# Attention in a hybrid decoder layer: the normalising multiplications of the probabilities on GpSimd instead of VectorE, and one of five value products in full f32 instead of two

## What is computed

```python
def masked_softmax(s, mask):
    s = jnp.where(mask, s.astype(jnp.float32), -jnp.inf)
    m = jnp.max(s, axis=-1, keepdims=True)
    m = jnp.where(jnp.isfinite(m), m, 0.0)
    e = jnp.exp(s - m)
    return e / jnp.maximum(jnp.sum(e, axis=-1, keepdims=True), 1e-30)
...
p_c = masked_softmax(s, cmp_end[None, :] <= t[:, None])
o_c = jnp.einsum('bgrqn,bgnd->bgrqd', p_c.astype(dt), cv)
...
o = (gates[..., 0:1] * unblock(o_c) + gates[..., 1:2] * unblock(o_s)
     + gates[..., 2:3] * unblock(o_w))
```

## Time and profile before

| | us |
|---|---|
| median of 3 runs (lowest, highest) | 1763.86 (1763.45, 1766.72) |
| the profiled execution | 1763.33 |
| its span from the first to the last instruction | 1761.2 |
| TensorE busy, of the span | 1649.9 (94%) |
| VectorE busy | 1049.6 (60%) |
| ScalarE busy | 630.3 (36%) |
| GpSimd busy | 90.7 (5%) |

### The profile page before, as it was taken

The page is one execution under the profiler, slowest core; times in us unless marked ns, Lnnn a source line. Parts: engine busy times, 40 slices in busy tenths (PEclk is TensorE's granted clock), DMA queues, the critical chain, the costliest instruction groups (busy, mean ns, idle before and its releaser), DMA issues.

```text
span 1761.2 us, 22256 instructions
## 1 busy us (share of the span) xinstructions
PE 1649.9 (94%) x8157; PEld 1334.5 (76%) x8157; DVE 1049.6 (60%) x2098; ACT 630.3 (36%) x1177; POOL 90.7 (5%) x126
## 2 busy tenths in 40 slices
PE   8899999997789999989899999999999999997894
PEld 6688888897656767668688888888888888876673
DVE  6734556655899999732555555555555555555233
ACT  5215344345677777621422122122122122113121
POOL 0101211220000000001000000000000000000002
PEclk9899999997899999999999999999999999998997
DMA  5433232234000000230212112112112112102002
GB/s 191 137 97 114 95 116 89 70 120 159 22 16 17 18 4 1 96 108 1 96 38 71 36 36 72 36 36 72 36 36 72 36 36 72 48 0 96 0 36 83
DMA packets 49002, 110.57 MB, mean 63 GB/s; under 512 B 8992, under 2 KB 17184, under 8 KB 48928
## 3 DMA queue, kind: packets, MB, share of 16 engines
q1 hardware_dynamic: 41504, 85.47, 14.8%
q0 software_dynamic: 7424, 24.12, 4.1%
HBM read 89.65 MB, written 19.92 MB: 62 GB/s over the span
## 4 chain that ended last, share of the span: by engine, by line
PE 80%; DVE 9%; ACT 3%; issue 2%; DMA 2%; POOL 0%; POOLq 0%; DVEq 0%; SPq 0%; ACTq 0%
PE ps L1360 28%; PE ps L1035 13%; PE ps L1036 12%; PE ps L1037 12%; PE ps L1181 3%; PE ps L1297 3%; PE ps L1254 2%; PE ps L1260 1%; PE ps L1204 1%; PE ps L1299 1%; DVE htl L1674 1%; PE ps L1040 1%; PE ps L1300 1%; DVE mx L1724 1%; DMA out<-ost 1%
## 5 line engine op out<-in xcount | busy, mean ns | idle before, releaser
L1860 DVE TENSOR_TENSOR h<-h,ps 128x512 f32<-128x512 f32 x352 | 236.4, 686 | 157.0 <-PE ps L1037 155.3
L1360 PE MATMUL ps<-hth,wuh 128*128 128x512 f32 x704 | 218.8, 392 | 3.1 <-DVE wul L1674 3.1
L1360 PE MATMUL ps<-htl,wuh 128*128 128x512 f32 x704 | 218.7, 392 | 0.0
L1360 PE MATMUL ps<-hth,wul 128*128 128x512 f32 x704 | 218.5, 392 | 0.0
L1035 PE MATMUL ps<-wh,xth 128*128 128x512 f32 (+1 forms) x448 | 186.7, 417 | 14.9 <-DVE wl L1456 13.3
L1037 PE MATMUL ps<-wh,xtl 128*128 128x512 f32 (+1 forms) x448 | 170.8, 381 | 0.0
L1036 PE MATMUL ps<-wl,xth 128*128 128x512 f32 (+1 forms) x448 | 170.3, 380 | 0.0
L976 ACT ACTIVATE ffh<-ffa 128x1024 fp32r<-128x1024 f32 x22 | 23.3, 1060 | 385.1 <-DVE ffa L1877 385.1
L1360 PEld LDWEIGHTS ps<-hth,wuh 128*128 128x128 f32 x704 | 132.6, 189 | 33.0 <-issue 3.3
L1360 PEld LDWEIGHTS ps<-hth,wul 128*128 128x128 f32 x704 | 132.4, 188 | 29.3
L1360 PEld LDWEIGHTS ps<-htl,wuh 128*128 128x128 f32 x704 | 132.5, 188 | 28.8
(11 more groups left out here) (263 smaller groups left out, 3155.6 us busy)
## 6 DMA issues: line engine op xcount, KB each, us to landing
wuraw<-in_w_up SPq DMA_DIRECT2D x44, 512.0 KB, 5.3
wraw<-in_w_in SPq DMA_DIRECT2D x48, 256.0 KB, 3.3
proj_d<-stage POOLq DMA_DIRECT2D x48, 256.0 KB, 2.3
wdraw<-in_w_down SPq DMA_DIRECT2D x22, 512.0 KB, 3.5
rin<-proj_d POOLq DMA_DIRECT2D x32, 256.0 KB, 4.3
xraw<-in_xt SPq DMA_DIRECT2D x16, 256.0 KB, 5.8
h<-in_x SPq DMA_DIRECT2D x1, 4096.0 KB, 12.5
owraw<-in_w_out SPq DMA_DIRECT2D x16, 256.0 KB, 3.2
```

The lines of the kernel that those rows point to most:

```text
L1360: mm = nc.tensor.matmul(ps[:, 2 * part + half, :], w_, x_[:, k, half * 512:(half + 1) * 512], start=(k == 0 and i == 0), stop=(k == NK - 1 ...
L1860: nc.vector.tensor_tensor(hh, hh, ps[:, 4 + o_ % 4, :], ALU.add).then_inc(dn_add, 1)
```

## The change

Guard and reciprocal stay on VectorE; the reciprocal now signals GpSimd through a semaphore of its own count (`inv_done`, a reuse of `red_done`, which stands at 2 when attention begins) and waits until GpSimd has finished the slot four before, because its result has four buffers. The three multiplications move, in the same form, to a loop on GpSimd. And `whole` now holds for j % 5 of 0 alone: 36 tiles are whole and 112 are split.

```diff
--- before.py
+++ after.py
@@ -378,6 +378,7 @@
         tr_full, tr_h, tr_l = sem("tr_full"), sem("tr_h"), sem("tr_l")
         qk_done, nb_done, exp_done, norm_done, pv_done = (
             sem("qk_done"), sem("nb_done"), sem("exp_done"), sem("norm_done"), sem("pv_done"))
+        inv_done, INV0 = red_done, 2
         swap_done, csum_done, nsah_done, nsal_done = sem("swap_done"), sem("csum_done"), sem("nsah_done"), sem("nsal_done")
 
         h_in, wfb_in = sem("h_in"), sem("wfb_in")
@@ -441,7 +442,7 @@
 
 
 
-            return st[0] == "turn_p" and st[2] % 5 in (0, 2)
+            return st[0] == "turn_p" and st[2] % 5 == 0
 
         outs_of = {(v, j): n for n, (v, j) in enumerate(st[1:] for st in plan if st[0] == "output")}
 
@@ -673,6 +674,26 @@
                     if s * NK + k == RET0 - 4:
                         ret_load(0)
                     ret_slots(s, k, table)
+
+            def normalize(v, i):
+
+                n, (t, g_), (r_, br) = 2 * RG * v + i, divmod(v, G), divmod(i, 2)
+                m, hd = n % 4, g_ * RG + r_
+                pool.wait_ge(inv_done, INV0 + n + 1)
+                pr = prob[:, v % 2, r_]
+                if br == 0:
+                    p_ = pr[:, 0:(t + 1) * P]
+                    nc.gpsimd.tensor_scalar(p_, p_, rd2[:, m, 0:1], gates[:, t, hd, 1:2], ALU.mult, ALU.mult).then_inc(norm_done, 1)
+                else:
+                    p_ = pr[:, S:S + (t - max(0, t - WIN_T) + 1) * P]
+                    nc.gpsimd.tensor_scalar(p_, p_, rd2[:, m, 0:1], gates[:, t, hd, 2:3], ALU.mult, ALU.mult)
+                    at = S + (WIN_T + 1) * P
+                    p_ = pr[:, at:at + NCMP]
+                    nc.gpsimd.tensor_scalar(p_, p_, rd2[:, m, 1:2], gates[:, t, hd, 0:1], ALU.mult, ALU.mult).then_inc(norm_done, 1)
+
+            for v in range(NV):
+                for i in range(2 * RG):
+                    normalize(v, i)
 
             for t in range(NT):
                 pool.wait_ge(hms_done, t + 1)
@@ -1735,26 +1756,12 @@
                 return mark(nc.vector.tensor_scalar(rd[:, n % 4, 0:w], den[:, n % 4, 0:w], 1e-30, None, ALU.max))
 
             def invert_sum(v, i, guarded):
-                m, w = (2 * RG * v + i) % 4, 1 + i % 2
+                n, w = 2 * RG * v + i, 1 + i % 2
+                m = n % 4
                 dve.wait_ge(dve_chain, guarded)
-                return mark(nc.vector.reciprocal(rd2[:, m, 0:w], rd[:, m, 0:w]))
-
-            def normalize(v, i, inverted):
-
-                n, (t, g_), (r_, br) = 2 * RG * v + i, divmod(v, G), divmod(i, 2)
-                m, hd = n % 4, g_ * RG + r_
-                dve.wait_ge(dve_chain, inverted)
-                pr = prob[:, v % 2, r_]
-                if br == 0:
-                    p_ = pr[:, 0:(t + 1) * P]
-                    nc.vector.tensor_scalar(p_, p_, rd2[:, m, 0:1], gates[:, t, hd, 1:2], ALU.mult, ALU.mult).then_inc(norm_done, 1)
-                else:
-                    width = (t - max(0, t - WIN_T) + 1) * P
-                    p_ = pr[:, S:S + width]
-                    nc.vector.tensor_scalar(p_, p_, rd2[:, m, 0:1], gates[:, t, hd, 2:3], ALU.mult, ALU.mult)
-                    at = S + (WIN_T + 1) * P
-                    p_ = pr[:, at:at + NCMP]
-                    nc.vector.tensor_scalar(p_, p_, rd2[:, m, 1:2], gates[:, t, hd, 0:1], ALU.mult, ALU.mult).then_inc(norm_done, 1)
+                if n >= 4:
+                    dve.wait_ge(norm_done, n - 3)
+                nc.vector.reciprocal(rd2[:, m, 0:w], rd[:, m, 0:w]).then_inc(inv_done, 1)
 
             def p_low(st):
                 at = place_of[st]
@@ -1796,11 +1803,9 @@
                 if n < 2 * RG * NV:
                     exp_bias(*divmod(n, 2 * RG), maxima)
                 if 0 < n <= 2 * RG * NV:
-                    inverted = invert_sum(*divmod(n - 1, 2 * RG), guarded)
+                    invert_sum(*divmod(n - 1, 2 * RG), guarded)
                 for st in lows:
                     {"turn_p": p_low, "turn_ret": ret_low}[st[0]](st)
-                if 0 < n <= 2 * RG * NV:
-                    normalize(*divmod(n - 1, 2 * RG), inverted)
                 for st in slot:
                     {"split_q": q_split_low, "sum": add_parts, "combine": nsa_low}.get(st[0], skip)(st)
```

## The result

The changed kernel took 1775.9 us (median of 4 runs, 1775.1 to 1777.7), the kernel before 1764.2 us beside it: a ratio of 1.0065 (95% interval 1.0048 to 1.0083). It is slower by some 12 us, where 14 us faster were forecast, and outside the forecast's range of 1741 to 1768 us. The profiled execution of the changed kernel has a span of 1773.1 us.

A forecast was written before the change was run, and what follows sets the result against it. VectorE was taken to bound the stage up to t = 3, TensorE from t = 4; -13.9 - 1.0 + 2.7 - 0.6 - 1.6 - 6.4 + 6.4 + 1.3 = -13.1 us from 1763.3 gave 1750 us, range 1741 to 1768.

The forecast's parts named there:

- part 2: Thirty tiles from whole to split: TensorE saves 0.40 us each, VectorE pays +2.7 us on the path, buffer sharing costs nothing.
- that cover is gone: If TensorE's 1.8 us for two tiles does not hide the buffer wait, about 0.3 us per pair of split tiles.
- What bounds the kernel now: In the attention stage, a shorter VectorE pays up to t = 3; from t = 4 on only a shorter TensorE does.
- Part 1: Multiplications leave VectorE: 88.0 us of its busy time, on the path 13.9 us at t = 1 to 3 and 1.0 later.
- Part 3: Price of a multiplication on GpSimd: 0.7 us fixed plus 1.05 ns a column, 210 us in all, so GpSimd follows.
- Part 4: Border between units, transposes wait for GpSimd's last multiplication: +6.4 us for 8 units up to t = 3, +1.3 in the last.
- 5.9 us net: Gain on the path from splitting thirty tiles: TensorE's savings of 0.6, 1.6 and 6.4 us against VectorE's added 2.7 us.
- Rival 1: VectorE's small steps at t = 1 to 3 collide with GpSimd over SBUF access: 9 us, 1759 us; chance 0.20.
- Rival 2: GpSimd becomes the bound at t = 0 to 4 with 1.28 us fixed cost: slower, 1791 us; chance 0.15.
- Rival 3: No change: score-to-exponential loop latency sets t = 1 to 3, about 5 us lost to shared split-tile buffers: 1761 us; chance 0.12.

The follow-up runs named there:

- runs 3 and 4: Three buffers for split tiles, one for whole: in the changed kernel, 1751.0 us; in the kernel before with only the new tile split, 1767.8 us.
- run 1: Changed kernel with the old tiles (j % 5 of 0 and 2 whole), so only the multiplications move to GpSimd: 1762.5 us, ratio 0.9975.
- run 8: Changed kernel with three buffers for split tiles and one for whole ones, measured again on another occasion: 1749.6 us, ratio 0.9903.
- run 12: Changed kernel with three buffers for split tiles and only j % 10 of 0 whole (24 whole, 124 split): 1744.1 us, ratio 0.9876.
- run 6: Changed kernel with three buffers for split tiles and each unit's last-slot multiplications back on VectorE: 1749.4 us, ratio 0.99.
- run 10: Changed kernel, still two buffers, with the value product of tile j - 2 ahead of the transposes of tile j on TensorE: 1761.5 us, ratio 0.9974.
- run 7: Changed kernel with three buffers for split tiles and each bank's first score matmul issued twice for t = 0 to 2: 1753.5 us, ratio 0.9928.

## Why the prediction was wrong

**The step that failed is in part 2:** "four split tiles now follow one another and share two buffers, so the third copy waits for the first product. I cost that at nothing where 0.90 us a tile hides it". It costs 26 to 28 us (runs 3 and 4). I named the wait and then sized it by TensorE's time for two tiles, as if they followed one another. They do not: in the slots up to t = 3 there is at most about one tile a slot, and between the tile whose copy needs the buffer and the product that frees it lie the scores of a slot. They in turn wait for exponentials, and on ScalarE those stand behind the copy. The text asked what the copy waits for and not what is queued behind it. The price "if that cover is gone, about 0.3 us per pair of split tiles" was too small by the same step: 43 waits of 1.2 us in the mean. Some of the 26 to 28 us is a lower clock of TensorE that came with the waits, 3 to 4 us of it at t = 2 by the estimate of the last section.

**What bounds the kernel now.** Right in outline: TensorE from t = 4 on, VectorE up to t = 3. But a chain names the last releaser and not how close the next one is. With VectorE relieved, t = 2 and 3 together became 3.5 us shorter (run 1), not the 10.3 us that the multiplications' shares of the chain came to there.

**Part 1, -13.9 - 1.0 us.** Too large: run 1 gives 4 us by its median. Part of the rest went to the clock, below. VectorE's busy time fell by 69.0 us and not by 88.0, as records of neighbours overlap and I had added their durations: L1754 lasts until 457.21 and L1757 starts at 457.12, and 0.09 us for each of 192 records makes some 17 us. That the same move is worth 19 us where VectorE has more to do (runs 3 and 4) fits a gain that is set by how far VectorE stood above the next limit.

**Part 2, 0.40 us a tile for TensorE.** Confirmed: from run 1 to run 8, t = 4 to the end, 20 tiles, the stretches shrink by 1.9 + 1.5 + 1.3 + 1.9 = 6.6 us, 0.33 us each, and run 12 gives 0.37 to 0.40 us.

**Part 3, the price on GpSimd.** Too high in both parts. The groups by shape of the changed kernel:

```profile
L689 POOL TENSOR_SCALAR prob<-prob,rd,gates 128x640 f32<-128x640 f32 x32 | 28.0, 876 | 60.2 <-DVE rd L1764 60.2
L692 POOL TENSOR_SCALAR prob<-prob,rd,gates 128x63 f32<-128x63 f32 x64 | 26.1, 408 | 0.0
L686 POOL TENSOR_SCALAR prob<-prob,rd,gates 128x1024 f32<-128x1024 f32 x8 | 9.6, 1196 | 14.5 <-DVE rd L1764 14.5
...
L686 POOL TENSOR_SCALAR prob<-prob,rd,gates 128x640 f32<-128x640 f32 x8 | 7.0, 877 | 15.5 <-DVE rd L1764 15.5
```

The slope is (1196 - 877) / 384 = 0.83 ns a column, and 877 - 640 x 0.83 leaves 0.35 us fixed, where 1.05 ns and 0.7 us had been taken. In all it is 125 us and not 210. By the Trainium skill, GPSIMD Engine Reference, section 4.1, one-input operations are roughly line-rate; as an estimate, one column a cycle at the 1.2 GHz that its section 1 gives would be 0.83 ns, and the trace agrees. The under 0.1 us of fixed part, which the prediction had worked out from the two-input add of section 3.1, is too low for this instruction: the trace has 0.35 us.

**Part 4, the border, +6.4 + 1.3 us.** Hardly there. A unit's first transposes do wait for GpSimd in the changed kernel, 0.26 to 0.57 us in four places up to the start of t = 4 and 1.38 us in the last unit. Without that wait the kernel is not faster by anything that its time shows (run 6); in the last unit the hand-over costs some 0.5 us and not 1.3.

**The sum without the buffers.** For three buffers, where the cost left out in part 2 is absent, the forecast of 1750.2 us is near the 1751.0 and 1749.6 us measured. That is luck in part: the gain of part 1 was too high, the border, which is hardly there, made up for some of it, and the split gives more than was counted. From run 1 to run 8 it gives 0.0072 in the ratio, 12.7 us, where 5.9 us net were forecast; 4.7 of them lie at t = 1, where the profile of run 1 has its longest half clock.

**The rivals.** Rival 1 is refuted in its price and not in its mechanism. The small steps of VectorE last as long in the mean as before: the guard of two columns 161 ns in both kernels, the bias 169, the reciprocal 166. But only some eight of these 384 steps meet a GpSimd record at all, as GpSimd is mostly through before the next guard comes. Run 1 shows what happens where they meet. The subtraction of two SBUF tiles into nsal takes 0.72 us beside a GpSimd record and 0.41 us without. One bias of two columns takes 0.30 us, while a guard of one column (L1756) inside the same GpSimd record keeps its 0.14 us:

```profile
552.85 0.87 POOL L686 TENSOR_SCALAR prob<-prob,rd,gates 128x640 f32<-128x640 f32 x1 [2.65 <-DVE rd L1764]
553.27 0.72 DVE L1695 TENSOR_TENSOR nsal<-comb,nsah 128x256 fp32r<-128x256 f32 x1
...
572.41 0.41 DVE L1695 TENSOR_TENSOR nsal<-comb,nsah 128x256 fp32r<-128x256 f32 x1
```

```profile
492.18 0.41 POOL L692 TENSOR_SCALAR prob<-prob,rd,gates 128x63 f32<-128x63 f32 x1
492.19 0.14 DVE L1756 TENSOR_SCALAR rd<-den 128x1 f32<-128x1 f32 x1
492.31 0.30 DVE L1751 TENSOR_SCALAR nb<-mx 128x2 f32<-128x2 f32 x1
```

GpSimd is through at 553.72 and the subtraction 0.27 us later; the subtractions at 637.86 and 685.13 are 0.72 us long too and end 0.27 and 0.26 us behind GpSimd. So what SBUF — State Buffer of the Trainium skill, section Who interferes with whom, says of a shared port pair that is held for a whole instruction agrees with this trace. In all it lengthens nsal by 1.3 us in run 1 (500 ns in the mean where it was 420, 16 times) and by next to nothing in the changed kernel (422 ns). Rival 2 is refuted by the price. Rival 3 had the right place, "lost to the shared buffers of split tiles", and the right direction, with a fifth of the size.

## What to carry to other kernels

When a change alters which items share a buffer, count in the program's order what stands between the item that takes the buffer and the one that gives it back, on both engines: a wait costs what is queued behind it, and here a copy that waited for its buffer held up exponentials that could have gone ahead. The order alone can take the wait away, as run 10 did, but it moved a wait to the product. Relieving a busy engine is worth what lies between it and the next limit, so it pays most together with the edit that would load it again: 4 us alone, 19 us with thirty more subtractions. Three buffers instead of two for the item that has become frequent, and one instead of two for the rare one, cost 2 KB a partition and turned 12 us slower into some 16 us faster.

## What the runs showed of the hardware

TensorE's granted clock falls from 1.00 to 0.50 (from 2.4 to 1.2 GHz) for some microseconds in these stretches, and where it does so differs from kernel to kernel and from run to run. GpSimd only, 457 to 478 us (t = 1):

```profile
457.00:460.00 3.00, 2.09 (x17) 1.66 (x17) 2.92 (x14) 2.54 (x8) 0.98 (x3) 1.00 0.04 5
460.00:466.00 6.00, 4.75 (x25) 4.34 (x25) 3.15 (x16) 3.84 (x15) 2.94 (x6) 0.56 0.06 19
466.00:472.00 6.00, 6.00 (x15) 3.26 (x14) 2.31 (x14) 2.28 (x10) 2.05 (x4) 0.50 0.00 0
472.00:478.00 6.00, 5.89 (x27) 4.74 (x26) 4.41 (x18) 4.53 (x13) 1.49 (x3) 0.52 0.20 66
```

TensorE was busy 2.09 of 3 us before it fell. At half the clock it is full, 6.00 of 6 us with 15 matmuls, and VectorE is busy for 2.31 of them. Before, the clock stands at 1.00 from 456 to 727 us, though TensorE was busy only 1.40 of 3 us from 457 to 460. The changed kernel has such dips too, 484 to 487 us and about 498 to 504 us, in the stretch that lost most. What they cost can be estimated from the one kernel that was profiled twice: three buffers has some 10 us at half clock in t = 1 the first time and 3 the second, and took 26.6 and 24.2 us, about a third of a microsecond for each microsecond at half clock. By that estimate 3 to 4 us of the changed kernel's loss at t = 2 are the clock's, with some 10 us at half clock, and about 6 us of GpSimd only at t = 1, with 17. The runs of GpSimd only agree: six of eleven have a mean clock of 0.970 and 1762.5 to 1763.6 us, the four at 0.974 or 0.975 have 1755.6 to 1759.4. That it falls because TensorE pauses more often when VectorE is faster is argued, not shown; run 7 did not settle it.
